# Third layer's mixers: who applies the convolution taps, where the transposes and the pooling stand, and when the gates' operands are split

## The reference, cut to what matters

```python
u = _rmsnorm(h, mix_norm_g)
p_pool, p_bval, p_bgate, p_cgate, p_cx = jnp.split(u @ w_in, splits, axis=-1)   # 256, 256, 256, 512, 512
# pooling: running means over 2, 4, 8, 16 tokens minus the token, then a 64x64 product a group
y_a = _pool_mixer(p_pool, pool_w, pool_scale)
# conformer: gate, causal convolution of 31 taps, layer norm over 256 channels, silu, product
u = v * jax.nn.sigmoid(gt); u = _causal_depthwise_conv(u, w_dw, b_dw)
y_b = jax.nn.silu(_layernorm(u, ln_g, ln_b)) @ w_pw
# gated linear recurrence over 512 channels, with a causal convolution of 4 taps
xc = _causal_depthwise_conv(x_in, conv_w, conv_b)
r = sigmoid(xh @ w_a + b_a); i = sigmoid(xh @ w_x + b_x)
log_a = -8 * r * softplus(-lam); a = exp(log_a); mult = sqrt(-expm1(2 * log_a))
y_c = gelu(gate_in) * _linear_scan(a, mult * (i * xc))
h = h + concatenate([y_a, y_b, y_c]) @ w_out
```

## Time and profile before

| what | us |
|---|---|
| median of 3 runs | 3408.99 |
| lowest, highest | 3405.41, 3409.62 |
| the profiled execution | 3411.5 |
| its span | 3409.4 |

### The profile page before, as it was taken

How to read it: one execution, slowest core, us unless ns; L and a number is a source line. 1 busy time by engine, 2 the same in 40 slices (tenths; PEclk the granted TensorE clock), 3 DMA queues, 4 the chain that set the end, 5 groups by cost and what they waited for, 6 DMA issues and landing times.

```text
span 3409.4 us, 36687 instructions
## 1 busy us (share of the span) xinstructions
PE 3166.6 (93%) x14623; PEld 2608.9 (77%) x14623; DVE 2136.7 (63%) x2787; ACT 1374.5 (40%) x1941; POOL 1079.4 (32%) x485
## 2 busy tenths in 40 slices
PE   7999887889999999969999999998967899999997
PEld 2888776777888888767788888887855688888886
DVE  4625577576777776675756565554975665555554
ACT  4311587344333333442633333345446443333332
POOL 0101465144444442322444433420760022222320
PEclk9999999999999999989999999998987999999999
DMA  6435211212223232111111111111120111111111
GB/s 222 144 116 180 79 47 44 81 39 79 99 100 103 100 101 79 40 37 38 37 50 50 50 50 51 67 51 47 32 84 19 44 50 62 50 50 56 50 56 56
DMA packets 190995, 237.86 MB, mean 70 GB/s; under 512 B 9671, under 2 KB 149562, under 8 KB 190826
## 3 DMA queue, kind: packets, MB, share of 16 engines
q1 hardware_dynamic: 173338, 172.90, 16.3%
q0 software_dynamic: 9136, 32.22, 2.5%
q10 hardware_dynamic: 8352, 30.41, 2.5%
HBM read 218.70 MB, written 16.79 MB: 69 GB/s over the span
## 4 chain that ended last, share of the span: by engine, by line
PE 76%; DVE 12%; ACT 7%; issue 3%; DMA 1%; POOL 0%; SPq 0%; DVEq 0%; ACTq 0%; POOLq 0%
PE psum L610 25%; PE psum L611 24%; PE psum L612 24%; DVE page_r L621 2%; DVE small L1373 2%; ACT temp L913 1%; DVE PT_lo L621 1%; DVE small L743 1%; ACT page_r L616 1%; ACT prob L1339 1%; ACT U_hi L616 1%; DVE H L1478 1%; DMA page<-in_ada_w_dram 1%; DVE U_lo L621 1%; PE psum L789 1%
## 5 line engine op out<-in xcount | busy, mean ns | idle before, releaser
L610 PE MATMUL psum<-U_hi,page_r 128*128 128x512 f32 x2108 | 837.3, 397 | 28.0 <-DVE U_lo L621 19.2
L611 PE MATMUL psum<-U_lo,page_r 128*128 128x512 f32 x2108 | 830.5, 394 | 0.0
L612 PE MATMUL psum<-U_hi,page_r 128*128 128x512 f32 x2108 | 829.9, 394 | 0.0
L621 DVE TENSOR_TENSOR page_r<-page,page_r 128x1024 fp32r<-128x1024 f32 (+2 forms) x239 | 351.0, 1474 | 380.1 <-ACT page_r L616 378.1
L616 ACT CAST page_r<-page 128x1024 fp32r<-128x1024 f32 (+2 forms) x323 | 337.2, 1047 | 400.3 <-DVE page L641 110.1
L610 PEld LDWEIGHTS psum<-U_hi,page_r 128*128 128x128 f32 x2108 | 401.9, 191 | 123.0 <-DVE U_lo L621 23.7
L612 PEld LDWEIGHTS psum<-U_hi,page_r 128*128 128x128 f32 x2108 | 401.7, 191 | 85.5
L611 PEld LDWEIGHTS psum<-U_lo,page_r 128*128 128x128 f32 x2108 | 402.3, 191 | 81.6
L2035 ACT ACTIVATE temp<-psum 128x512 f32<-128x512 f32 x192 | 114.7, 597 | 856.0 <-PE psum L612 811.6
L610 PE MATMUL psum<-page_r,act_page_r 128*128 128x512 f32 x1176 | 457.5, 389 | 0.0
L611 PE MATMUL psum<-page_r,act_page_r 128*128 128x512 f32 x1176 | 457.5, 389 | 0.0
(11 more groups left out here) (344 smaller groups left out, 4801.1 us busy)
## 6 DMA issues: line engine op xcount, KB each, us to landing
page<-in_mlp_w_dram SPq DMA_DIRECT2D x128, 512.0 KB, 4.1
page<-in_ada_w_dram SPq DMA_DIRECT2D x48, 512.0 KB, 4.9
page<-in_w_in_dram SPq DMA_DIRECT2D x38, 512.0 KB, 3.9
page<-in_w_up_dram SPq DMA_DIRECT2D x32, 512.0 KB, 4.1
page<-in_w_down_dram SPq DMA_DIRECT2D x32, 512.0 KB, 4.1
ada_land<-in_ada_w_dram ACTq DMA_DIRECT2D x24, 512.0 KB, 4.4
sum_page<-in_ada_w_dram ACTq DMA_DIRECT2D x12, 512.0 KB, 5.5
act_page<-in_ada_w_dram ACTq DMA_DIRECT2D x12, 512.0 KB, 8.7
```

The source lines that it names most:

```text
L610: pe.matmul(out, l_hi, r_hi, start=start, stop=False, skip_group_check=read_between)
L611: pe.matmul(out, l_hi, r_lo, start=False, stop=False, skip_group_check=read_between)
L612: return pe.matmul(out, l_lo, r_hi, start=False, stop=stop, skip_group_check=read_between)
L621: return dve.tensor_tensor(lo, src, hi.bitcast(F32), ALU.subtract).then_inc(*k.lo.inc(*key))
```

## The change

All taps of both groups go to VectorE, in the order of `TAP_ORDER`: eight of group 0, then the two groups by turns; `TAPS_BEHIND` deals them behind units 2 to 10. ScalarE and GpSimd have none. The softplus polynomial moves from behind unit 3 to behind unit 1. The transposes stand ahead of units 12 and 13 (`pe_turn_taps`, `pe_turn_back`), measuring and normalising behind unit 11, SiLU into `dw` behind unit 12. Units 8 and 9 stay in SBUF, in `cx` and `work`, and are pooled in place, 0 behind unit 10 and 1 behind unit 11; only GELU's rows go to DRAM, from the temporaries. VectorE now casts the pooled rows' high part itself. The splits of `xc[0]` and `xc[1]` move ahead of the mixed rows' splits, those of `xc[2]` and `xc[3]` between the first heads' steps. ScalarE takes the heads two by two, and squares `a` in place of VectorE. `RG_TURNS` is now VectorE's alone, and TensorE's gates follow `GATES_AT`.

```diff
-FIRST_TAP = 3
+TAP_ORDER = [(t, 0) for t in range(8)] + \
+    [(t + 8 * (1 - g), g) for t in range(CONV_K) for g in (1, 0) if t + 8 * (1 - g) < CONV_K]
+TAPS_BEHIND = {2: 8, 3: 8, 4: 6, 5: 6, 6: 6, 7: 6, 8: 9, 9: 9, 10: 4}
+GATES_AT = {0: 0, 1: 1, 5: 2, 6: 3}
...
+RG_LAST = (("root", 3), ("scan", 2), ("scan", 3))
... pe_mixers, in the loop over IN2_ORDER
+        if (m, c) == (12, 0):
+            pe_turn_taps(k, pe, on)
+        if (m, c) == (13, 0):
+            pe_turn_back(k, pe, on)
... act_mixers
+        elif POOLED <= m < GELU:
+            on.wait_ge(*k.dve_done.at("xc", 3))
+            act.copy(columns_of(pooled_of(k, m - POOLED), 0, c), in2_bank(k, m, c)).then_inc(*k.taken.inc("in2", m, c))
+        elif m >= GELU:
+            t = k.act_temp.take(on, ("gelu", m, c), (k.gelu_out[k.act_temp.n % 3], (m, c)))
+            act.activation(k.temp[t][:], in2_bank(k, m, c), ACT.Gelu_apprx_tanh).then_inc(*k.taken.inc("in2", m, c))
-        for tap in taps(m, 3):
-                act.activation(k.temp[t][:], src[:, tap + h * CH:tap + (h + 1) * CH], ACT.Copy, scale=w)
         act_weights(k, act, on, at + 5 + m)
+        if m == 11:
+            normed_taps()
+        if m == 12:
+                    act.activation(k.dw[j][:, c * CH:(c + 1) * CH], k.bank("back", c, j), ACT.Silu, ...)
+    rows(0)
+    rows(1)
+    act_rg(k, act, on, "xc", 0)
+    mixed(0)
+    act_rg(k, act, on, "xc", 1)
+    mixed(1)
     act_weights(k, act, on, k.first["out2"] + 3)
... act_out2
+    for first in (0, 2):
+        for what in ("gates", "rates", "root", "y"):
+            for j in (first, first + 1):
+                act_rg(k, act, on, what, j)
+            if first == 0 and what == "rates":
+                act_rg(k, act, on, "xc", 2)
+                act_rg(k, act, on, "xc", 3)
+            if first and what == "gates":
+                act_weights(k, act, on, at + 4)
... dve_mixers; dve_mixers ends like act_mixers, with rows, xc and mixed by turns
-        for tap in taps(m, 4):
-            src, dst, w = k.gated[0], k.dw[0], k.columns("convb_dw_w_2", 2 * tap)
+        for tap, g in taps(m):
+            src, dst, w = k.gated[g], k.dw[g], k.columns("convb_dw_w_2", 2 * tap + g)
         dve_weights(k, dve, on, at + 5 + m)
+        if m == 10:
+            pooling(0)
+        if m == 11:
+            for pair in range(TPC):
+                on.wait_ge(*k.pe_done.at("dw", pair))
+                    dve_measure(...)
+            for t in range(TT):
+                dve_scale(k, dve, on, P, False, "dw", t)
+            pooling(1)
+    def rows(c):
+        u_free_of_in2(k, on, c)
+        for i in range(2):
+            dve.tensor_copy(hi, pooled_of(k, i)[:, s]).then_inc(*k.dve_done.inc("pooled high", i, c))
+            dve.tensor_tensor(lo, pooled_of(k, i)[:, s], hi.bitcast(F32), ALU.subtract)
+        for j in range(2):
+            dve_lo(k, dve, on, k.U_lo[:, c, 2 + j, :], k.dw[j][:, c * CH:(c + 1) * CH], k.U_hi[:, c, 2 + j, :], "z", c, j)
... pool_mixers
-                pool.tensor_tensor(k.dw[1][:, s], k.dw[1][:, s], v[:], ALU.add)
+            pool.dma_start(k.d_gelu[m - GELU][:, c * CH:(c + 1) * CH], k.temp[t][:])
```

More of the change, by code:

```diff
@@ L2503 @@
 IN2 = 14
+POOLED = 8
 GELU = 10
@@ L2586, in pe_mixers @@
         k.freed[k.unit("in2", m).s] = k.up_done, ("post3", ("in2", m), NCH - 1)
[L2588 to L2607, removed]
     small = k.unit("small")
     on.wait_ge(*k.lo.at("w", small.s))
[L2612 to L2621, removed]
     for c in range(NCH):
@@ L2630, in pe_mixers, with pe_gates @@
         last.then_inc(*k.pe_done.inc("pointwise", c))
[L2631 to L2636, removed]
+        for i in range(2):
+            hi, lo = y_part(k, i, c)
+            on.wait_ge(*k.lo.at("pooled", i, c))
+            n = k.banks.take(on, ("group", i, c), (k.taken, ("group", i, c)))
+            three_passes(pe, k.psum[:, n, :], small.hi[:, i * P:(i + 1) * P], small.lo[:, i * P:(i + 1) * P], hi, lo,
+                         True, True).then_inc(*k.pe_done.inc("group", i, c))
+    k.freed[small.s] = k.pe_done, ("group", 1, 1)
+def pe_gates(k, pe, on, j):
     rg = k.unit("rg")
@@ L2671, in act_mixers, with normed_taps @@
     act.activation(k.meta_hat[:], k.meta_raw[:], ACT.Identity, bias=bias, scale=scale).then_inc(*k.hat_ok.inc("meta"))
+    def normed_taps():
+        for pair in range(TPC):
+            if pair >= 2:
+                k.act_temp.take(on, ("dw", pair), (k.pe_done, ("back", pair)))
+            for i in range(2):
+                act_root(k, act, on, P, "dw", 2 * pair + i)
+            for i in range(2):
+                scale, bias = scale_bias(k, P, False, "dw", 2 * pair + i)
+                on.wait_ge(*k.scaled.at("dw", 2 * pair + i))
+                s = slice(2 * i * P, 2 * (i + 1) * P)
+                last = act.activation(dw_temp(k, pair)[:, s], k.bank("dw", pair)[:, s], ACT.Identity, bias=bias,
+                                      scale=scale)
+            last.then_inc(*k.taken.inc("dw", pair))
     for m, c in IN2_ORDER:
@@ L2734, in group, with mixed @@
+    def rows(c):
+        u_free_of_in2(k, on, c)
+        for j in range(2):
+            on.wait_ge(*k.taken.at("z", c, j))
+            act_hi(k, act, on, k.U_hi[:, c, 2 + j, :], k.dw[j][:, c * CH:(c + 1) * CH], "z", c, j)
+    def mixed(c):
+        on.wait_ge(*k.pe_done.at("pointwise", c))
+        for j in range(2):
+            act_hi(k, act, on, k.U_hi[:, c, 2 + j, :], k.bank("pointwise", c, j), "u", "y", c, 2 + j)
+        for i in range(2):
             t = k.act_temp.take(on, ("group", i, c), (k.lo, ("u", "y", c, i)))
@@ L2762, in act_rg @@
     w_r, w_t, w_a = rg_work(k, j)
-    if what == "gates":
+    if what == "xc":
+        on.wait_ge(*k.dve_done.at("xc", j))
+        on.wait_ge(*k.up_done.at("meta", GELU - 1))
+        u_free_of_in2(k, on, NCH - 1)
         for c, at, size in RG_PARTS:
             act_hi(k, act, on, y_part(k, 4 + j, c)[0], k.xc[j][:, at:at + size], "xc", j, c)
+    elif what == "gates":
         rg_work_free(k, on, j)
@@ L2934, in dve_mixers @@
                    2 + j)
+        for i in range(2):
+            dve_lo(k, dve, on, k.U_lo[:, c, i, :], k.temp[k.act_temp.of("group", i, c)][:], k.U_hi[:, c, i, :], "u", "y",
+                   c, i)
+    rows(0)
+    rows(1)
+    dve_rg(k, dve, on, "xc", 0)
+    mixed(0)
+    dve_rg(k, dve, on, "xc", 1)
+    mixed(1)
     dve_weights(k, dve, on, k.first["out2"] + 3)
```

300 lines of the change are left out of this document (131 added, 169 removed).

## The result

The changed kernel takes 3362.36 us (median of 4 runs, 3360.23 to 3364.13), the kernel before 3409.3 beside it (4 runs, 3405.41 to 3415.0): a ratio of 0.9865, 95% interval 0.9853 to 0.9877. The profiled execution took 3362.28 us with a span of 3360.0. The forecast was 3362.

A forecast was written before the change was run, and what follows sets the result against it. A serial chain over VectorE, ScalarE and GpSimd was taken to bound the third layer's mixers. First out21 add at 2633.5 instead of 2680.4 gains 47 us: 3411.5 becomes 3364.5, less 2.5 gives 3362 (3352 to 3374, 63%).

The forecast's parts named there:

- Taps: VectorE's 62 taps beside the units: 1.28 us each with GpSimd silent, last ending near 2495, 3 us early.
- Transposes: Around unit 12: 16 forward (3.4 us) from 2498.2, 16 back (4.4 us); unit 13 ends at 2527.8, 7.8 us later.
- Rows of y: Behind unit 13: TensorE rests 6.7 us, first pointwise product at 2534.5 instead of 2564.1.
- First two heads: Heads 0 and 1: scan turns of 6.9 us, TensorE waits 6 to 8 us for banks, reaching G = 2601.
- A: As a time: ScalarE's last sigmoid of gates 1, 2557.5. As a rival: taps stay at 1.97 us, 3421 us; 4%.
- G: Time of the sigmoids of gates 3: A+41.3 and 2 us for the half clock, 2601.
- Last two heads: From G: two scan turns 13.8 us, three weight splits 3.7; first out21 addition at G+32.5 = 2633.5.
- B: Rival: batched heads leave TensorE at half clock and queues wait for each other, 20 us lost, 3382 us; 15%.
- C: Rival: more is won, from the bank wait (8 us), half clock (2) and earlier rows of y (5), 3347 us; 15%.
- D: Rival: taps or banks stall TensorE in the units and the gain is given back, within 0.2%; 3%.

The follow-up runs named there:

- additions: Changed kernel plus 48 back-to-back GpSimd additions of two SBUF operands from unit 2's end on; TensorE waited 26.5 us; 3398.35 us, ratio 0.9975.
- fills: Changed kernel plus 90 GpSimd zero fills of a scratch tile, reading nothing, from unit 2's end on; 3361.06 us, ratio 0.9864.
- the additions ahead of the scans: Changed kernel with VectorE adding out20's tiles 2 and 3 ahead of scans 0 and 1; 3358.45 us, ratio 0.9859.

## Why the prediction was right, and where its terms were off

The forecast (3362, one of 63%) named the mechanism and nearly the time. By its own steps, with 1.3 us taken from the times of after in brackets, as that trace runs behind by so much at unit 4 (ScalarE's last copy there starts at 2408.49 for 2407.18):

- *Taps.* 1.28 us each was taken, 1279 ns is measured as the length of a row; from one tap to the next it is 1.21 where the groups take turns and 1.31 within a group; the last ends at 2495.8 (2494.5), "near 2495". TensorE never waits in the units. The additions and fills show the reason, rather than the three quiet taps of the earlier trace rows alone.
- *Transposes.* They start at 2499.39 (2498.1), where 2498.2 was said. But they cost 1.66 and 2.27 us to the next pass (the first row is 1.91 long), not 3.4 and 4.4: I took the price from the earlier trace rows, where TensorE had rested for 9.64 us and ran at half clock, and put it where it had not rested. This is the largest error, 3.9 us of 7.8. Unit 13 ends at 2525.4 (2524.1) for 2527.8. In the experiment where TensorE waited 26.5 us the same sixteen took 3.65.
- *Rows of y.* The wait is 5.86 us for 6.7; the first pointwise pass at 2531.30 (2530.0) for 2534.5.
- *First two heads.* A is 2555.6 (2554.3) for 2557.5. ScalarE's and VectorE's order, as worked out, held: scan 0 ended at A+20.2 (A+20.9), the bank wait was 5.94 ("6 to 8"), but G came at A+42.0 for A+43.5.
- *Last two heads.* First out21 addition at G+33.3 for G+32.5, so 2630.95 (2629.7) for 2633.5. The scan turns are 6.82 and 6.90 us (6.9), the weight splits behind them as said:

```profile
2610.07 1.24 DVE L2992 TENSOR_TENSOR xc<-xc,gated 128x1040 f32<-128x1040 f32 x1 [0.34 <-ACT gated L2802]
...
2616.89 1.24 DVE L2992 TENSOR_TENSOR xc<-xc,work 128x1040 f32<-128x1040 f32 x1
...
2623.97 4.63 DVE L620 TENSOR_TENSOR page_r<-page,page_r 128x1024 fp32r<-128x1024 f32 x4 [0.17 <-ACT page_r L615]
2630.95 1.37 DVE L1477 TENSOR_TENSOR H<-H,psum 128x512 f32<-128x512 f32 x2 [2.36 <-PE psum L611]
```

  These rows are VectorE's timeline of the changed kernel and answer to the earlier trace rows: two scan turns, then the splits, then the first addition, with TensorE's first pass at 2625.25 between.
- *The sum.* 47 us were forecast for this event; it is 50.7 in the stretch. The median run moved by 46.9 only: the rest of the profiled execution was 1.5 us longer than before's, and its time of 3362.28 is nearly the median, so the 2.5 us that I took off was not there. That the forecast is off by 0.4 us only is luck: 3.7 us too little gain in the stretch, against 2.5 us taken off for nothing and the 1.5 us by which the rest ran longer.

The rivals: A did not happen, and the additions show what a reading GpSimd would have cost. B (half clock and queues) took nothing of its 20 us, the clock being 0.93 up to 2576, though 0.79 behind it. The prediction has the higher clock only inside its times and not as a term; in the stretch it is 16.7 of the 50.7 us. Of C, the wait for banks stayed (5.94 us), and the rows of y straight behind unit 13 were not in this change but can be had: 6.8 us in the stretch. Of D, nothing was given back in the units.

## What to carry to other kernels

Before a term is priced, look whether the row it comes from follows a rest of TensorE: the row of the same sixteen transposes is 1.91 us long in a busy stretch and 3.40 and 3.65 behind waits of 9.64 and 26.54 us. Where GpSimd only adds up what another engine prepared, count its operands in SBUF: 48 additions cost this kernel 36 us, 90 fills nothing. In a serial chain over three engines, undo the parts one by one, as the sum of waits was 34.0 of the 50.7 us here; and before attacking a wait for banks, look whether the engine that frees them is itself in the chain: here a swap of its instructions only moved the wait.

## What the runs showed of the hardware that I had not expected

VectorE's one-input operation with a per-partition scalar is hit as well by GpSimd's additions: the 128x1040 multiply-add took 1.77 us beside them and 0.64 after their end (rows above), where the changed kernel has 0.64 to 0.82. Not each is hit: one of 128x1024 in the midst of the additions took 0.91. The fills slow it a little too, to at most 1.17. By the Trainium skill, SBUF — State Buffer, section "Who interferes with whom", such an operation can enter a mode that uses the port shared with GpSimd; the rows fit that. The kernel's stretch also began at full clock in two of the traces (the fills, and the additions ahead of the scans) and at half in the others (first pass 0.47 for 0.77 us). Their stretches are 1.9 and 1.0 us shorter than the changed kernel's, though the programs are the same up to there.
